# Weaving the sparse-attention indexer of blocks 1 to 3 into the feed-forward stage ahead of it, in a decoder-layer kernel on Trainium2

## The chip, the core and the metric

The kernel runs on one core of a Trainium2 chip. A core has five engines with a program each: PE (TensorE, matmuls), DVE (VectorE), ACT (ScalarE), POOL (GpSimd) and SP (SyncE, which issues the DMAs here). They run side by side and meet only at semaphores. The metric is the device time of one execution in microseconds (us), as the median of several.

## The reference

One decoder layer over 2048 prompt tokens and 64 sample tokens: RMSNorm and a combined projection; group A, sparse attention in which an indexer picks for each query its 256 best keys; group B, gated linear attention (GLA); an output projection; a SwiGLU feed-forward. What the change touches:

```python
# the indexer: a score for each query t and key s, from 8 index heads
dots  = jnp.einsum('bqhd,bsd->bqhs', iqs, idx_keys)
score = jnp.einsum('bqh,bqhs->bqs', iws, jax.nn.relu(dots))
score = jnp.where(key_pos <= tp, score, -jnp.inf)
_, sel = lax.top_k(score, topk)                  # topk = 256
# softmax attention over the picked keys gives attn_o
mix = jnp.concatenate([attn_o, gla_o], axis=-1)
x = x + jnp.einsum('btc,cd->btd', mix, w_out_l)
h = rmsnorm(x, ffn_g)
u = jax.nn.silu(jnp.einsum('btd,df->btf', h, wg)) * jnp.einsum('btd,df->btf', h, wu)
x = x + jnp.einsum('btf,fd->btd', u, wd)
```

D_MODEL is 1024, D_FF is 2816, and a head has 64 dimensions.

## The kernel before, in words

The 2048 prompt tokens are four blocks of 512 tokens, and a block is four tiles of 128 queries (tiles 0 to 15); the sample tokens are a fifth block. `SCHED` lists the stages, and every engine walks through it in its own program: P (projection), G (GLA), I (indexer), F (output projection and feed-forward), A (attention). The order is P0 G0 I0 A0, and then for b = 1 to 4: P(b) G(b) I(b) F(b-1) A(b), and F4 at the end. So block b's indexer stands just ahead of the feed-forward of block b-1, and the search for its top 256 keys runs on DVE while PE does that feed-forward.

**Stage I(b).** The scores of a tile are made in units: one index head and one chunk of up to 512 keys (`IU`). PE multiplies (two matmuls, lines 768 and 770, into one of 8 PSUM banks), ACT takes the relu (line 1142), DVE multiplies by the query's weight and adds to the row of scores (lines 1575 and 1577). Blocks 1, 2 and 3 have 64, 96 and 128 units. POOL then masks the diagonal (line 1852).

**The search.** The 256th largest score of each query is found bit by bit in 32 steps (`search_step`): a comparison with a running count for each tile (line 1344), then two small instructions for all tiles of the step (1347, 1350). `end_search` counts and ranks ties and turns the scores into an additive mask, in six instructions for each chunk of 512 keys (lines 1358 to 1376). A step takes all four tiles of the block at once. Some steps (`early_steps`) stand ahead of the norm in F, the rest behind it (`pick_block`). Tiles 2 and 3 alone are searched inside attention A0 (`late_picks`).

**Stage F(b).** O: 8 accumulations of 24 matmuls (the output projection, for one 128-row piece of the residual each) and the sum of squares for the norm. U: 44 accumulations of 24 matmuls (gate and up, in turn). D: 8 outputs of 66 matmuls. Weights come in fp32, and are split into two fp16 halves by ACT (`highs`, lines 1000 and 1002) and by POOL or DVE (`lows`, lines 1754 and 1312) into a ring of four tiles. In O ACT copies each result out of PSUM and POOL adds it to X (lines 1239, 1900). Between O and U the norm goes through ACT (970 to 974, 1249, 1253), DVE (1300 to 1306, 1608) and POOL (1906). U's products are put together by POOL (`gated`).

**Stage A(b).** For each tile and head (a unit, 32 in a block): logits on PE (810, 812), mask and maximum on DVE (1631, 1634), exp on ACT (1167), transposes and the product with V on PE (824, 835), scaling on DVE (1640, 1644). PE's `logits` runs one unit ahead and waits for DVE's mask after three banks. DVE gets to the first mask of A(b) only when it is through with the search; POOL waits for DVE's end of F.

The functions that the diff touches, and what calls them:

## Time and profile before

| what | us |
|---|---|
| median of 3 runs | 4000.27 (3999.38 to 4002.51) |
| the profiled execution | 4002.26 |
| its span in the trace | 4000.4 |
| PE busy | 3288.3 (82% of the span) |
| DVE busy | 2147.4 (54%) |
| ACT busy | 1824.1 (46%) |
| POOL busy | 1720.6 (43%) |

The profile is of one execution. Its stages, by PE's instructions, in us from the start of the span:

| block b | end of P(b) | first dots of I(b) | first accumulation of U in F(b-1) | end of D in F(b-1) | first mask of A(b) on DVE |
|---|---|---|---|---|---|
| 1 | 623.1 | 678.1 | 797.4 | 1148.0 | 1149.6 |
| 2 | 1422.6 | 1476.8 | 1620.6 | 1973.6 | 1975.3 |
| 3 | 2302.5 | 2357.5 | 2528.5 | 2881.2 | 2913.3 |

A busy share is an average over stages. What a change is worth is read from the stage in which it stands: from which engine was the last to be ready there.

### The profile page before, as it was taken

Reading aid. Unit: us, or ns where it says so; the run is one execution under the profiler, and the core shown is the slowest. Engines: PE = TensorE matmul, PEld = TensorE weight load, DVE = VectorE, ACT = ScalarE, POOL = GpSimd, SP = SyncE. Lnnn points to the kernel's source line nnn. Section 1 sums busy time; section 2 is a strip of 40 time slices with the busy share of each in tenths; the row PEclk is TensorE's granted clock in tenths of the full one; section 3 lists DMA queues with packets and bytes.
Section 4 is the critical chain, followed back from the end, with each engine's and each line's share of the span. In section 5 each row is a group of like instructions: output and inputs, shape, how many; then the busy total and the mean of one; then the engine's idle time right before and its main releaser. Section 6 shows DMA issues by size and latency. Waiting matters only on the chain.

```text
span 4000.4 us, 57257 instructions
## 1 busy us (share of the span) xinstructions
PE 3288.3 (82%) x19950; PEld 1844.1 (46%) x19950; DVE 2147.4 (54%) x3923; ACT 1824.1 (46%) x2702; POOL 1720.6 (43%) x1292
## 2 busy tenths in 40 slices
PE   3972597699989978799989968799879866999865
PEld 1451445244447452344476532344367742444455
DVE  3625663799115638899244648899944411100155
ACT  1331234555445346554464346554355514554356
POOL 2014202578654024676542033676621014776434
PEclk9995699899989999899999989899989957999766
DMA  2301031223220311232210201232210252232356
GB/s 84 93 25 42 6 98 36 63 89 105 85 86 30 99 35 58 74 100 82 76 64 22 93 27 53 69 105 85 78 35 1 96 157 93 90 103 83 104 188 217
DMA packets 112068, 313.08 MB, mean 78 GB/s; under 512 B 14035, under 2 KB 20515, under 8 KB 111747
## 3 DMA queue, kind: packets, MB, share of 16 engines
q1 hardware_dynamic: 111874, 310.63, 24.7%
q8 instruction: 106, 1.74, 0.2%
q14 instruction: 88, 0.71, 0.1%
HBM read 296.35 MB, written 14.24 MB: 78 GB/s over the span
## 4 chain that ended last, share of the span: by engine, by line
PE 58%; DVE 17%; issue 8%; ACT 5%; POOLq 4%; DMA 3%; POOL 2%; DVEq 2%; ACTq 0%; SPq 0%
PE bank L585 15%; PE bank L586 15%; PE bank L587 15%; DVE spare L1344 7%; PE bank L835 5%; PE bank L824 2%; DVE scores L1577 2%; DVE ring L1312 1%; ACT ring L1000 1%; DVE R L1631 1%; DMA kT<-in_w_gu 1%; ACT bank L1142 1%; POOL H L1906 1%; DVE miss L1347 1%; PE bank L810 1%
## 5 line engine op out<-in xcount | busy, mean ns | idle before, releaser
L585 PE MATMUL bank<-H,ring 128*128 128x512 f16 (+2 forms) x2560 | 855.2, 351 | 145.3 <-POOL H L1906 92.8
L586 PE MATMUL bank<-H,ring 128*128 128x512 f16 (+2 forms) x2560 | 855.1, 351 | 0.0
L587 PE MATMUL bank<-H,ring 128*128 128x512 f16 (+2 forms) x2560 | 854.4, 350 | 0.0
L1344 DVE TENSOR_SCALAR_CACHE_REDUCE spare<-scores,cand 128x640 uint8<-128x640 f32 (+4 forms) x448 | 662.5, 1479 | 43.5 <-issue 3.6
L1754 POOL TENSOR_TENSOR ring<-raw,ring 128x1024 f16<-128x1024 f32 (+1 forms) x252 | 488.2, 1942 | 290.1 <-ACT raw L1002 284.5
L1000 ACT ACTIVATE ring<-raw 128x1024 f16<-128x1024 f32 (+2 forms) x356 | 348.9, 980 | 386.2 <-PE bank L587 159.4
L585 PEld LDWEIGHTS bank<-H,ring 128*128 128x128 f16 (+1 forms) x2560 | 259.6, 102 | 407.6 <-issue 140.3
L587 PEld LDWEIGHTS bank<-H,ring 128*128 128x128 f16 (+1 forms) x2560 | 261.0, 103 | 246.5 <-issue 8.2
L586 PEld LDWEIGHTS bank<-H,ring 128*128 128x128 f16 (+1 forms) x2560 | 260.2, 102 | 242.8 <-issue 6.6
L1631 DVE CUSTOM_DVE_ANT_0 R<-bank,scores 128x512 f32<-128x512 f32 (+3 forms) x256 | 140.8, 592 | 383.1 <-PE bank L812 371.6
L585 PE MATMUL bank<-R,ring 128*128 128x512 f16 (+1 forms) x880 | 298.1, 354 | 37.8 <-POOL R L1927 25.6
L1264 ACT ACTIVATE mixA<-bank 128x512 f32<-128x512 f32 (+1 forms) x220 | 114.4, 520 | 464.4 <-PE bank L587 464.2
L835 PE MATMUL bank<-vtok,R 128*128 128x128 f32 x2176 | 286.1, 289 | 23.7 <-DVE R L1644 22.1
L586 PE MATMUL bank<-R,ring 128*128 128x512 f16 (+1 forms) x880 | 297.9, 354 | 0.0
L587 PE MATMUL bank<-R,ring 128*128 128x512 f16 (+1 forms) x880 | 297.7, 354 | 0.0
L835 PEld LDWEIGHTS bank<-vtok,R 128*128 128x128 f32 x2176 | 274.1, 205 | 27.1 <-issue 19.9
L1312 DVE SCALAR_TENSOR_TENSOR ring<-raw,ring 128x1024 f16<-128x1024 f32 x104 | 134.1, 1293 | 253.4 <-ACT ring L1000 252.3
L1178 ACT ACTIVATE R<-bank 128x512 f32<-128x512 f32 (+3 forms) x320 | 156.8, 530 | 196.8 <-PE bank L824 196.4
L1002 ACT ACTIVATE raw<-raw 128x1024 f32<-128x1024 f32 (+1 forms) x252 | 237.6, 943 | 0.0
L1000 ACT ACTIVATE ring<-kT 128x1024 f16<-128x1024 f32 (+2 forms) x189 | 181.1, 963 | 113.5 <-PE bank L587 69.1
L810 PE MATMUL bank<-kT,q 128*128 128x256 f16 (+3 forms) x384 | 128.8, 340 | 123.0 <-DVE mx L1631 95.3
L824 PE MATMUL bank<-cst,R 128*128 128x128 f32 x1088 | 166.4, 291 | 71.5 <-ACT R L1167 65.5
(299 smaller groups left out, 6013.8 us busy)
## 6 DMA issues: line engine op xcount, KB each, us to landing
raw<-in_w_gu SPq DMA_DIRECT2D x132, 512.0 KB, 3.6
raw<-in_w_in SPq DMA_DIRECT2D x104, 512.0 KB, 3.5
kT<-in_w_gu SPq DMA_DIRECT2D x88, 512.0 KB, 3.8
raw<-in_w_d SPq DMA_DIRECT2D x48, 384.0 KB, 3.1
X<-in_xT SPq DMA_DIRECT2D x8, 2048.0 KB, 9.3
raw<-in_w_d SPq DMA_DIRECT2D x48, 320.0 KB, 3.2
raw<-in_w_out SPq DMA_DIRECT2D x24, 512.0 KB, 3.5
kT<-in_w_d SPq DMA_DIRECT2D x32, 384.0 KB, 3.2
```

The costliest lines, as they stand in the source:

```text
L585: mm(o, lhs[0], rhs[0], start=first, stop=False)
L586: mm(o, lhs[0], rhs[1], start=False, stop=False)
L587: return mm(o, lhs[1], rhs[0], start=False, stop=last)
L810: mm(bank[n % 3][:, 0:kn], q[:, h, cq:cq + 128], kT[:, h // 4, 0, k0:k0 + kn], start=True, stop=False)
L824: last = nc.tensor.transpose(bank[3 + n % 2][:, 128 * (t % 4):128 * (t % 4) + 128], lg[:, u % 2, 128 * t:128 * t + 128], ident)
L835: last = mm(bank[5 + u % 2][:, 0:128], pT[:, u % 2, t, :], vtok[:, t, :], start=(t == 0), stop=(t == i))
L1000: last = A(ring[:, n % 4, 0, 0:cols], whole[:, 0:cols], ACT.Copy, scale=W_UP)
L1002: last = A(whole[:, 0:cols], whole[:, 0:cols], ACT.Copy, scale=W_UP)
L1312: v.scalar_tensor_tensor(ring[:, n % 4, 1, 0:cols], raw_at(n)[0][:, 0:cols], W_UP, ring[:, n % 4, 0, 0:cols], ALU.mult, ALU.subtract).then ...
L1344: v.tensor_scalar(flags[:, 0:128 * (i + 1)], row_of(i), cut_at[:, i % 4:i % 4 + 1], None, ALU.is_ge, ALU.add, accum_out=tally[:, i % 4:i % ...
L1631: v.tensor_tensor_reduce(lg[:, u % 2, k0:k0 + kn], bank[n % 3][:, 0:kn], m, 1.0 / Q_SCALE, OUTSIDE, ALU.add, ALU.max, mx[:, u % 2, c:c + 1 ...
L1754: g.tensor_tensor(ring[:, n % 4, 1, 0:cols], raw_at(n)[0][:, 0:cols], ring[:, n % 4, 0, 0:cols], ALU.subtract).then_inc(S("w_split"), 1)
```

## The change

For b = 1 to 3 the stage I(b) is gone from `SCHED`. Its units are spread over the accumulations of F(b-1), which is then called woven: a slot is one accumulation of O (8 slots) or U (44 slots), and behind each of the first slots stand three units (`I_NEXT`, `i_slot`), so that the 64, 96 and 128 units reach up to slot 21, 31 and 42. PE makes their dots behind the slot's accumulation (`dots_for`), now with 4 banks instead of 8; ACT takes the relu (`relus_for`), DVE adds (`adds_for`). O and the sum of squares move to banks 4 to 6. The loops over U are written out for this.

The output projection starts right after GLA. Its first four weight tiles are split in the projection stage (`p_ahead`). X is loaded when PE is through with G. DVE now adds the product to X itself and splits O's weights, and applies the gain together with the norm; ACT's copies and POOL's adds in O are gone. U's first accumulation takes its eight pieces of H one by one (`f_h` counts pieces).

The search takes two tiles at a time, then the other two; in block 3 two, one, one. A group's first step may stand only five slots after the one behind which its last unit was added. A plan with fixed costs (`SLOT_US`, `UNIT_PE_US`, `UNIT_DVE_US`, and a cost for each step) says how many steps stand behind each slot; what is left of the search follows after the last slot. Tile 15 gets 16 of its 32 steps there; the other 16 and its `end_search` stand between the units of A3. Stores of keys and values move into P, and some buffers get another place.

```diff
-EARLY_NS = 38000
-LATE_TILES = [2, 3]
+LATE_TILES = [2, 3, 15]
+LATE_STEP = 16
+SLOT_US, UNIT_PE_US, UNIT_DVE_US = 5.2, 0.43, 0.75
...
-            SCHED += [("P", b), ("G", b), ("I", b), ("F", b - 1), ("A", b)]
+            SCHED += [("P", b), ("G", b)] + [("I", b)] * (b == NBLK) + [("F", b - 1), ("A", b)]
...
+        I_NEXT = [{u: min(n0 + 3 * (u + 1), n1) for u in range(-1, KT + 36)}
+                  for n0, n1 in ((sum(i < 4 * b for i, _, _ in IU), sum(i < 4 * b + 4 for i, _, _ in IU))
+                                 for b in range(1, NBLK))]
+        def i_slot(b, slot):
+            return range(I_NEXT[b][slot - 1], I_NEXT[b][slot]) if slot < KT + 36 else range(0)
...
+            def dots_for(b, slot):
+                for n in i_slot(b, slot):
+                    i, c, h = IU[n]
+                    k0, kn = score_chunks(i)[c]
+                    cq = 128 * (i % 4)
+                    pe.wait_ge(S("i_added"), n - 3)
+                    mm(bank[n % 4][:, 0:kn], iq[:, h, cq:cq + 128], ikT[:, 0, k0:k0 + kn], start=True, stop=False)
+                    mm(bank[n % 4][:, 0:kn], iq[:, h, cq:cq + 128], ikT[:, 1, k0:k0 + kn], start=False, stop=True
+                       ).then_inc(S("i_dots"), 1)
...
+                    if woven(b):
+                        sp.wait_ge(S("end_pe"), nph)
+                        load_x(b, NT)
...
+                    for s in range(2 * NF if woven(b) else 0):
+                        w = weights_at(base["U", b] + s)
+                        pe.wait_ge(S("u_bank_free"), u0 + s + 1)
+                        for k in range(KT):
+                            if s == 0:
+                                pe.wait_ge(S("f_h"), KT * b + k + 1)
+                            last = three(bank[4 + s % 4][:, 0:NT], [w[e][:, 128 * k:128 * k + 128] for e in range(2)],
+                                         [H[:, e, k, 0:NT] for e in range(2)], k == 0, k == KT - 1)
+                        last.then_inc(S("products"), 1)
+                        dots_for(b, KT + s)
...
+            def search(b):
+                t = list(tiles_of(b))
+                groups = [t[0:2], t[2:4]] if b < NBLK - 1 else [t[0:2], t[2:3], t[3:4]]
+                for tiles in groups:
+                    done = max(n for n, u in enumerate(IU) if u[0] == tiles[-1]) + 1
+                    yield done, 0
+                    dve.wait_ge(S("i_diag"), tiles[-1] - 1)
+                    late = b == NBLK - 1 and tiles[-1] in LATE_TILES
+                    for n in range(LATE_STEP if late else STEPS):
+                        search_step(tiles, n)
+                        yield done, sum(128 * (i + 1) / 960 + 0.35 for i in tiles) + 0.5
+                    if not late:
+                        end_search(tiles)
+                        yield done, sum(128 * (i + 1) / 960 * 6 for i in tiles)
...
+                if kind == "F" and woven(b):
+                    start_search(tiles_of(b + 1))
+                    dve.wait_ge(S("x_in"), 16 * x_loads(nph))
+                    for dt in range(KT):
+                        dve.wait_ge(S("products"), base["O", b] + dt + 1)
+                        v.scalar_tensor_tensor(X[:, dt, :], bank[4 + dt % 2][:, :], 1.0 / (W_UP * M_UP), X[:, dt, :],
+                                               ALU.mult, ALU.add).then_inc(S("o_added"), 1)
+                        lows(base["O", b] + dt + 4)
+                        adds_for(b, dt)
+                    dve.wait_ge(S("f_root"), b + 1)
+                    newton(nF[0], nF[1], nF[2], nF[3], H_UP)
...
+                    for s in range(2 * NF):
+                        units = i_slot(b, KT + s)
+                        adds_for(b, KT + s)
+                        credit = min(credit + SLOT_US + (UNIT_PE_US - UNIT_DVE_US) * len(units), 2 * SLOT_US)
+                        while credit > 0 and I_NEXT[b][min(KT + s - 5, KT + 35)] >= ready:
+                            ready, cost = next(picks, (10 ** 6, 0))
+                            credit -= cost
+                    for _ in picks:
+                        pass
```

How the rows of the programs move, at the places that matter. First DVE's program of **before**, at the end of I3 and the start of the search for block 3 (tiles 12 to 15; a row is a line, an operation, what it writes and reads, its shape and how many in a row):

```order
L1575 TENSOR_SCALAR scores<-bank,iw 128x512
L1577 SCALAR_TENSOR_TENSOR scores<-bank,iw,scores 128x512 x7
L1337 MEMSET cand 128x4
L1344 TENSOR_SCALAR spare,tally<-scores,cand 128x1664
L1344 TENSOR_SCALAR spare,tally<-scores,cand 128x1792
L1344 TENSOR_SCALAR spare,tally<-scores,cand 128x1920
L1344 TENSOR_SCALAR spare,tally<-scores,cand 128x2048
L1347 TENSOR_SCALAR miss<-tally 128x4
L1350 SCALAR_TENSOR_TENSOR cand<-miss,cand 128x4
```

And the **changed** program of DVE around its first search step of block 3 (line 1465 or 1467 is an add, 1421 a comparison, 1424 and 1427 the two small ones):

```order
L1465 TENSOR_SCALAR scores<-bank,iw 128x512
L1421 TENSOR_SCALAR spare,tally<-scores,cand 128x1664
L1421 TENSOR_SCALAR spare,tally<-scores,cand 128x1792
L1424 TENSOR_SCALAR miss<-tally 128x2
L1427 SCALAR_TENSOR_TENSOR cand<-miss,cand 128x2
L1421 TENSOR_SCALAR spare,tally<-scores,cand 128x1664
L1421 TENSOR_SCALAR spare,tally<-scores,cand 128x1792
L1424 TENSOR_SCALAR miss<-tally 128x2
L1427 SCALAR_TENSOR_TENSOR cand<-miss,cand 128x2
```

Before, the first step follows the last of the 128 units. Now it follows unit 80 of 128 (behind the 19th accumulation of U), has half the tiles, and 47 more adds stand between the steps that follow.

On PE, the **changed** program at one of the slots of U (606 to 608 are the accumulation's matmuls, 627 and 628 the dots):

```order
L607 MATMUL bank<-H,ring 128x512
L608 MATMUL bank<-H,ring 128x512
L627 MATMUL bank<-ikT,R 128x512
L628 MATMUL bank<-ikT,R 128x512
L627 MATMUL bank<-ikT,R 128x512
L628 MATMUL bank<-ikT,R 128x512
L627 MATMUL bank<-ikT,R 128x512
L628 MATMUL bank<-ikT,R 128x512
L606 MATMUL bank<-H,ring 128x512
```

**Before**, the last dots of I3 stand directly ahead of the first matmuls of the output projection, and none stands in U:

```order
L768 MATMUL bank<-ikT,R 128x512
L770 MATMUL bank<-ikT,R 128x512
L768 MATMUL bank<-ikT,R 128x512
L770 MATMUL bank<-ikT,R 128x512
L585 MATMUL bank<-mixA,ring 128x512
L586 MATMUL bank<-mixA,ring 128x512
L587 MATMUL bank<-mixA,ring 128x512
```

On DVE in A3 the **changed** program has steps for tile 15 between the units (1748 and 1751 are a unit's mask and maximum, 1757 and 1761 the scaling):

```order
L1748 ISA R,mx<-bank,R 128x256
L1748 ISA mx 128x1
L1751 TENSOR_REDUCE nmax<-mx 128x1
L1757 RECIPROCAL rden<-den 128x1
L1761 TENSOR_SCALAR R<-bank,rden 128x64
L1421 TENSOR_SCALAR spare,tally<-scores,cand 128x2048
L1424 TENSOR_SCALAR miss<-tally 128x1
L1427 SCALAR_TENSOR_TENSOR cand<-miss,cand 128x1
L1748 ISA R,mx<-bank,scores 128x512
```

There are 16 such steps over the first 23 units of A3, and `end_search` for tile 15 stands behind the last of them, with the mask of unit 23 ahead of it and the mask of unit 24 behind it. The program of before has none of these.

## Rows read from the trace of the kernel before

**Rows 1.** Windows over U and D of F2, the gap and A3; busy us.

```profile
core 0: us, PE busy (x) PEld busy (x) DVE busy (x) ACT busy (x) POOL busy (x), PEclk, DMA share, GB/s
2528.50:2759.40 230.90, 230.86 (x1056) 103.97 (x1056) 218.82 (x227) 117.70 (x138) 166.84 (x106) 0.99 0.29 93
2759.40:2881.20 121.80, 116.69 (x529) 52.23 (x528) 115.62 (x120) 46.41 (x66) 79.02 (x54) 0.97 0.32 92
2881.20:2913.30 32.10, 1.37 (x7) 0.51 (x6) 28.88 (x46) 0.60 (x1) 3.94 (x4) 0.57 0.00 0
2913.30:3180.90 267.60, 234.65 (x1894) 196.13 (x1895) 109.84 (x419) 154.77 (x243) 50.19 (x75) 0.95 0.09 31
```

**Rows 2.** Windows from the end of the search to attention, blocks 1 and 2.

```profile
1015.10:1148.00 132.90, 127.75 (x583) 57.18 (x581) 0.01 (x1) 50.40 (x72) 80.74 (x60) 0.97 0.32 92
1918.90:1974.00 55.10, 54.73 (x254) 24.62 (x252) 0.00 (x0) 21.95 (x33) 35.18 (x26) 1.00 0.35 102
```

**Rows 3.** PE's timeline from GLA to I3: start, us, instruction, idle before.

```profile
2344.43 3.70 PE L751 MATMUL bank<-H,cst 128*128 128x512 f32 x8 [2.68 <-ACT H L1125]
2357.45 0.58 PE L768 MATMUL bank<-ikT,R 128*128 128x512 f16 x1 [9.32 <-ACTq L1291]
```

**Rows 4.** The page's DMA issues: size and us to landing of X.

```profile
X<-in_xT SPq DMA_DIRECT2D x8, 2048.0 KB, 9.3
```

**Rows 5.** Timeline of the norm between O and U in F2.

```profile
2517.63 10.58 POOL L1906 TENSOR_TENSOR H<-R,H 128x512 f16<-128x512 f32 x8 [10.54 <-ACT H L1253]
2528.54 0.61 PE L585 MATMUL bank<-H,ring 128*128 128x512 f16 x1 [21.10 <-POOL H L1906]
```

**Rows 6.** Groups by shape in I3: count, busy us, mean ns, idle before.

```profile
L1577 DVE SCALAR_TENSOR_TENSOR scores<-bank,iw,scores 128x512 f32<-128x512 f32 x91 | 68.3, 751 | 9.1 <-ACT bank L1142 0.9
```

**Rows 7.** DVE groups by shape in block 3's search (2462 to 2914).

```profile
L1344 DVE TENSOR_SCALAR_CACHE_REDUCE spare<-scores,cand 128x2048 uint8<-128x2048 f32 x32 | 75.1, 2346 | 3.1
L1344 DVE TENSOR_SCALAR_CACHE_REDUCE spare<-scores,cand 128x1664 uint8<-128x1664 f32 x32 | 62.3, 1946 | 2.9
L1347 DVE TENSOR_SCALAR miss<-tally 128x4 int32<-128x4 f32 x32 | 26.9, 839 | 2.5
L1344 DVE DVE_READ_ACCUMULATOR spare<-scores,cand 128x1 f32 x128 | 10.7, 84 | 0.0
L1350 DVE SCALAR_TENSOR_TENSOR cand<-miss,cand 128x4 int32<-128x4 int32 x32 | 5.2, 163 | 2.4
```

**Rows 8.** DVE groups by shape in block 2's search (1554 to 1919).

```profile
L1350 DVE SCALAR_TENSOR_TENSOR cand<-miss,cand 128x4 int32<-128x4 int32 x32 | 21.0, 656 | 2.4
L1347 DVE TENSOR_SCALAR miss<-tally 128x4 int32<-128x4 f32 x32 | 15.4, 480 | 2.5
```

**Rows 9.** DVE groups by shape in A0 (318 to 492), with its late search.

```profile
L1350 DVE SCALAR_TENSOR_TENSOR cand<-miss,cand 128x1 int32<-128x1 int32 x64 | 13.1, 204 | 5.5 <-issue 0.8
L1347 DVE TENSOR_SCALAR miss<-tally 128x1 int32<-128x1 f32 x64 | 9.8, 154 | 4.9
```

**Rows 10.** All 160 instances of line 1347: duration ns min/median/max, first and last start.

```profile
L1347 DVE TENSOR_SCALAR miss<-tally x160: 153/170/1895, 321.0 to 2815.6; 128x4 int32<-128x4 f32 x96, 128x1 int32<-128x1 f32 x64
```

**Rows 11.** Windows over `end_search` of blocks 1, 2 and 3.

```profile
946.50:1015.10 68.60, 68.60 (x320) 31.09 (x319) 65.72 (x57) 36.41 (x43) 59.12 (x34) 1.00 0.28 91
1837.90:1918.90 81.00, 75.16 (x339) 33.48 (x338) 76.79 (x81) 28.79 (x43) 53.00 (x34) 0.96 0.30 82
2817.10:2912.80 95.70, 65.47 (x304) 29.37 (x301) 89.96 (x105) 24.48 (x35) 48.41 (x31) 0.86 0.22 64
```

**Rows 12.** DVE's timeline at the end of block 3's `end_search`, POOL silent.

```profile
2908.09 0.69 DVE L1376 SCALAR_TENSOR_TENSOR scores<-spare,scores 128x512 f32<-128x512 f16 x1
2912.05 0.69 DVE L1376 SCALAR_TENSOR_TENSOR scores<-spare,scores 128x512 f32<-128x512 f16 x1
```

**Rows 13.** DVE's timeline in A3: the first mask of a unit.

```profile
3051.64 0.69 DVE L1631 CUSTOM_DVE_ANT_0 R<-bank,scores 128x512 f32<-128x512 f32 x1 [4.63 <-PE bank L812]
```

**Rows 14.** A window just after the start of A3.

```profile
2918.00:2922.00 4.00, 3.01 (x13) 2.62 (x14) 0.31 (x3) 2.54 (x5) 0.72 (x1) 0.50 0.00 0
```

265 lines of the change are left out of this document (162 added, 103 removed).

## The prediction

> **What bounds the kernel now.** I read the windows by stage first, since the busy shares of the page mix stages with different limits. U and D of F2 are PE's: 230.9 and 121.8 us long, with PE busy for 230.86 and 116.69 of them [rows 1]. 44 accumulations in 230.9 us make 5.25 us each, and 1056 matmuls make 0.22 us each. At the end of D the blocks differ. In blocks 1 and 2 DVE is through with its search 132.9 and 55.1 us before attention starts, and PE is the last [rows 2]. In block 3 it is the other way round: between 2881.2 and 2913.3 PE does next to nothing and DVE is busy for 28.88 of 32.10 us [rows 1]. So the search has a slack of 133 us in block 1, 55 in block 2, and none (minus 32) in block 3. The change takes time out of PE's path and delays the search, so the question is which of the two arrives last at the start of A1, A2 and A3. I count both from the first dots of I(b), as before has them: 678, 1477 and 2357.5.
>
> **PE's path.** GLA ends on PE at 2344.4 + 3.7 = 2348.1, and the next matmul waits until 2357.45 for ACT [rows 3]. The first O accumulation now fills this gap (5.25 us; I add 1 us for the four weight tiles that are split at the end of the projection). Only then come dots, from 2358.5. A unit is two matmuls, 0.44 us, so a full slot is 5.25 + 1.3 = 6.55 us. X is asked for only when GLA is over on PE and lands 9.3 us later [rows 4], and DVE's first adds queue behind X and behind a weight split; PE then waits some 4 us for bank 0. With 8 sums of squares at 0.9 us the last sum is done at about 2416.5. Between it and U's first accumulation stands the norm: PE waits 21.1 us, the last 10.58 of them for POOL's eight subtractions [rows 5]. Now U starts after the first of these, and its first accumulation lasts as long as they do, so the second starts at about 2439. That is 81.5 us behind the old first dots; I use this for all three blocks (before, the second accumulation of U starts at 2533.8).
>
> From there 43 accumulations take 226 us, and the units that stand in U from its second slot on (37, 69, 101) take 16, 30 and 43 us. DVE's lumps of steps hold PE back a little in the slots with units (a slot's units wait for the adds of the slot before): I take 10 us. With D at 121.8 us, D ends at 678 + 81.5 + 226 + 16 + 10 + 121 = 1132 (before 1148), at 1477 + 81.5 + 226 + 30 + 10 + 122 = 1947 (before 1973.6) and at 2357.5 + 81.5 + 226 + 43 + 10 + 122 = 2840 (before 2881.2). PE alone would gain 16, 27 and 41 us, and block 3's gap of 32 on top.
>
> **DVE's path.** The group rule decides. The first pair's last unit is number 32, 48 and 64 of the block; three in a slot and five slots of distance put the first step behind slot 15, 20 and 26, which is U's accumulation 7, 12 and 18 (counted from 0). At 6.55 us a slot, and 1.5 us for relu and add, the search starts at 807, 1639 and 2557. Before, it started at 731, 1554 and 2462, just behind the last unit: it is 76 to 95 us later, and 16, 33 and 47 units still have to be added among the steps. A 512-wide add is 0.751 us [rows 6], with gaps 0.8 to 0.84: 13, 26 and 40 us. Where the steps run in between, DVE waits for nothing, so what it has to do simply adds up:
>
> A comparison takes 1.946 us for 1664 keys and 2.346 for 2048, with 0.084 for the count's read and 0.1 of gaps [rows 7]: 0.133 us for each 128 keys and 0.4. The two small instructions cost 0.839 + 0.163 in block 3 [rows 7] and 0.656 + 0.480 in block 2 [rows 8], with gaps 1.16 and 1.29 us a step; in A0, where POOL does little, 0.204 + 0.154 [rows 9], with gaps 0.52. They don't get cheaper with two tiles, and there are now 64 (block 3: 80) instead of 32 in a block. `end_search` of a whole block took 68.6, 81.0 and 95.7 us [rows 11]; with POOL silent a chunk of 512 keys takes 3.96 us [rows 12], about 6 otherwise.
>
> Block 1: adds 13, steps 32 x (2.27 + 1.29) = 114 and 32 x (2.80 + 1.29) = 131, ends 69: 327 us, from 807 to 1134. This meets PE at 1132.
> Block 2: adds 26, steps 32 x (3.33 + 1.29) = 148 and 32 x (3.86 + 1.29) = 165, ends 81: 420 us, from 1639 to 2059. After 1947 POOL is silent: 14 steps at 0.77 us less and a cheaper second end (28 for 41) give back 24; POOL's thinner load in the longer slots another 5. So 2030.
> Block 3: adds 40, 32 steps of tiles 12 and 13 at 4.4 + 1.16 = 178, their end 55: 273 us, to 2830; tile 14: 3 steps at 3.55 and 29 at 2.93, to 2925; its end 4 x 3.96 + 2.7 = 19, to 2944; 16 steps of tile 15 at 2.53 + 0.52, to 2993. Less 5 for POOL's thinner load: 2988.
>
> **Attention.** A(b) starts with the later of the two: A1 at 1133 instead of 1149 (-16), A2 at 2030 instead of 1975.3 (+55), A3 at 2988 instead of 2913.3 (+75). Inside A3 DVE waits 4.63 us in a unit for PE's logits [rows 13], so a step of 3.05 us hides in it. `end_search` for tile 15 does not: 2.4 + 0.3 + 16 = 19 us in one unit, and PE runs only one unit ahead. Less the 4.6 of idle time: +14. If the steps did not hide, they would cost up to 49 more; if PE's lead hid the end too, 0. In the I stages that go, ACT, POOL and SP have nothing on the path that sets the end: their work is hidden by PE's slots of 6.55 us (ACT has 117.70 us in 44 of U's slots [rows 1], 2.7 us each, and three relus more, each no longer than an add).
>
> The clock adds little. In A3's first microseconds it was 0.50, which is the lower level of 1.2 GHz, after 32 us without matmuls [rows 14]; A2 now starts after a gap too, and half speed over the 4 us of that row costs 2 us.
>
> **Sum.** -16 + 55 + 75 + 14 + 2 = +130, against the profiled execution's 4002.3 (span 4000.4): 4132. The median of the runs is 2 us lower than that execution: 4130.
>
> **A rule that bears on the sum.** The small TENSOR_SCALAR of line 1347 took between 153 and 1895 ns, with a median of 170 [rows 10], the long ones beside POOL's work. The Trainium skill, page "SBUF — State Buffer", section "Who interferes with whom", says that a VectorE tensor_scalar in a 2-port mode and a GpSimd instruction exclude each other, the later one waiting for the whole of the other, whereas the form that writes its accumulator doesn't take part. This speaks against splitting the search into more steps. By the rule's worst case each step beside POOL waits for a whole instruction of it, which is the upper bound of the next sentence; by its best case, lucky order, none does, which is rival A.
> By rows alone: 50 steps of block 2 and 35 of block 3 lie beside POOL, and between the mean (0.48 to 0.84) and the longest (1.895) there is 1.4 and 1.06 us each, +108. To the other side, with POOL's cover gone (0.52 a step and 3.96 a chunk), block 2 would be 38 + 13 us shorter and block 3 22 + 18: -91. I take the means, since DVE met the same engine in the same stage.
>
> **Rivals.**
> A. Steps and ends at their quiet price (0.52 us, 3.96 a chunk), because the woven slots let DVE and POOL pass each other. A2 starts at 1979, A3 at 2948: 4039. For it: POOL's share of U falls from 166.84 of 230.9 us [rows 1], 0.72, to 0.60 with longer slots. Against it: 0.60 is nearer to 0.72 than to silence. 8%.
> B. Faster: DVE keeps up, and PE's D is last in every block. That gives -16, -28, -73 at the starts and +14 in A3: 3897. It is decided at one place: block 3's search has to be over by 2840, 283 us after its start, against 431 of work; it would need steps before unit 64's slot plus five, which the program doesn't have, or adds that run much earlier than PE's slots. 4%.
> C. The steps in A3 don't hide, since PE's wait of three banks is shorter than a step, and each costs its 3.05 us; or the first of the lumps hold PE longer in U: 16 x 3.05 = +49, 4179. For it: DVE's 109.84 us in A3 [rows 1] would grow by 68, and PE, busy for 234.65 of 267.6, has little room of its own. Against it: the 4.63 us of idle time [rows 13]. 10%.
> D. No change that a measurement can tell (0.2%, 8 us, is about the limit): block 2 and 3 lose no more than block 1 and the stage I give back. Nothing in the rows leads there. 2%.
>
> **How the numbers follow.** The forecast has 76%, with 4095 to 4165 as its own range (10 us on each of three DVE paths, and A3's end between 0 and 25). The range for 8 in 10 reaches down towards A and up to C: 4060 to 4180. Faster by over 0.2%: B alone, 4%. Within: 2%. Slower: the rest, 94%.
>
> **What would show it.** The profile after should have: the second accumulation of U 82 us behind the old place of the first dots; the first comparison of a block at U's accumulation 7, 12, 18; no gap of PE before A1, one of about 83 us before A2 and one of about 148 before A3, with DVE busy in both; line 1424 at a mean over 0.4 us while POOL works and under 0.2 in the gaps; in A3 DVE's idle time before the mask gone in 16 units, PE's waits unchanged there, and one stall of about 15 us at tile 15's `end_search`. I am wrong if the gaps are missing, if DVE idles while a search is open, or if U's slots are much longer than 6.6 us.

## The result and the profile after

| | before | after |
|---|---|---|
| median of 4 runs, us | 4001.39 (3999.38 to 4004.81) | 4148.02 (4137.35 to 4178.49) |
| ratio of the means, 95% interval | | 1.0378 (1.032 to 1.0436) |
| profiled execution, span | 4002.3, 4000.4 | 4178.49, 4176.0 |

The changed kernel is slower by 3.8%, inside the range (4060 to 4180) and 18 us above the forecast of 4130; the profiled execution, the slowest of the four, lies just inside too. The stages of the profiled execution after, as the table of before has them:

| block b | end of P(b) | start of U's second accumulation in F(b-1) | first comparison | end of D in F(b-1) | first mask of A(b) on DVE |
|---|---|---|---|---|---|
| 1 | 644.2 | 799.2 | 844.9 | 1165.5 | 1167.1 |
| 2 | 1440.3 | 1581.2 | 1660.2 | 1981.1 | 2047.4 |
| 3 | 2371.3 | 2528.3 | 2644.2 | 2926.3 | 3060.4 |

The windows of after (start:end, length, then busy us of PE, PEld, DVE, ACT and POOL, PE's granted clock, DMA) are in order: the gap before A2; stage G of block 3; U of F2 from its first dots (they stand behind the first accumulation, 0.3 us ahead of the second) to its last; D of F2; the gap before A3; and the masks of A3.

```profile
1981.10:2047.40 66.30, 1.16 (x7) 0.51 (x6) 60.31 (x95) 0.60 (x1) 4.04 (x4) 0.53 0.00 0
...
2383.80:2430.70 46.90, 37.49 (x162) 30.93 (x162) 12.25 (x38) 4.92 (x11) 0.00 (x0) 0.50 0.00 1
2528.00:2757.80 229.80, 220.60 (x1026) 99.05 (x1025) 141.22 (x191) 133.29 (x207) 135.18 (x88) 0.99 0.23 77
2809.60:2926.30 116.70, 116.67 (x528) 52.19 (x528) 109.23 (x128) 44.55 (x63) 74.82 (x51) 0.98 0.32 92
2926.30:3060.40 134.10, 1.36 (x7) 0.52 (x6) 121.75 (x191) 0.60 (x1) 3.70 (x4) 0.52 0.00 0
3060.40:3321.90 261.50, 213.15 (x1572) 176.23 (x1573) 158.49 (x490) 137.17 (x212) 47.19 (x70) 0.91 0.04 14
```

Against [rows 1]: the gap of 32 us before A3 has become one of 134, and block 2, which had none [rows 2], has one of 66. In both PE and POOL do next to nothing, and DVE is busy for over nine tenths: the search is what the others wait for. Block 1 has no gap (1165.5 to 1167.1). The masks of A3 took 231.6 us before and take 261.5 now.

**The account.** The two profiled executions differ by 176 us. One part is the clock of stage G, between the projection and the indexer. Its state updates, a chain of small float32 matmuls, took 30.4 us in all four blocks of before, at a granted clock of 1.00. In after they took 46.9 us in blocks 0, 1 and 3, at 0.50, and 32.8 in block 2, at 0.89, since the clock rose to 1.00 inside it. That is 3 x 16.5 + 2.4 = 52 us. I take it out by counting, for each block, the time from the end of P(b) to the first mask of A(b), less what G(b) took over 30.4 us:

| from the end of P to attention, less G's excess | block 1 | block 2 | block 3 | masks of A3 | G's excess, blocks 0 to 3 |
|---|---|---|---|---|---|
| before | 526.5 | 552.7 | 610.8 | 231.6 | 0 |
| after | 506.4 | 604.7 | 672.6 | 261.5 | 51.9 |
| difference | -20 | +52 | +62 | +30 | +52 |

The sum is 176. The same numbers are given below for each experiment, since the profiled execution shows in which blocks G ran at half clock, and the other runs behind a median don't.

### The profile page after: what moved, and what is told of

Its sections match the earlier page's. It is cut to its first block, busy times and chain, and to the rows that moved or that the text cites. A ratio compares the mean times of both kernels' runs of the same rounds, so it can differ in the third digit from the quotient of the medians.

```text
span 4176.0 us, 56774 instructions
## 1 busy us (share of the span) xinstructions
PE 3331.4 (80%) x19950; PEld 1900.8 (46%) x19950; DVE 2283.0 (55%) x4243; ACT 1721.2 (41%) x2591; POOL 1624.7 (39%) x1232
## 4 chain that ended last, share of the span: by engine, by line
PE 53%; DVE 25%; issue 8%; ACT 4%; DMA 3%; POOLq 3%; DVEq 2%; POOL 2%; ACTq 1%; SPq 0%
PE bank L606 12%; PE bank L608 12%; PE bank L607 12%; DVE spare L1421 12%; PE bank L867 4%; PE bank L856 2%; DVE ring L1389 2%; DVE miss L1424 2%; DVE scores L1467 2%; DVE cand L1427 1%; DVE R L1748 1%; DMA kT<-in_w_gu 1%; ACT ring L1054 1%; POOL H L2032 1%; DVE spare L1446 1%
## 5 line engine op out<-in xcount | busy, mean ns | idle before, releaser
L1421 DVE TENSOR_SCALAR_CACHE_REDUCE spare<-scores,cand 128x640 uint8<-128x640 f32 (+8 forms) x448 | 662.3, 1478 | 41.5 <-issue 1.8
L1871 POOL TENSOR_TENSOR ring<-raw,ring 128x1024 f16<-128x1024 f32 (+1 forms) x216 | 411.8, 1910 | 299.2 <-ACT raw L1056 293.3
L1389 DVE SCALAR_TENSOR_TENSOR ring<-raw,ring 128x1024 f16<-128x1024 f32 x140 | 200.5, 1435 | 348.2 <-ACT ring L1054 347.1
L1998 POOL TENSOR_TENSOR R<-scores,near_bias 128x256 f32<-128x256 f32 (+1 forms) x128 | 92.2, 722 | 490.1 <-DVE nmax L1751 217.6
L1467 DVE SCALAR_TENSOR_TENSOR scores<-bank,iw,scores 128x512 f32<-128x512 f32 (+3 forms) x252 | 172.2, 683 | 153.9 <-ACT bank L1070 135.3
```

The source lines that it names most:

```text
L1389: v.scalar_tensor_tensor(ring[:, n % 4, 1, 0:cols], raw_at(n)[0][:, 0:cols], W_UP, ring[:, n % 4, 0, 0:cols], ALU.mult, ALU.subtract).then ...
L1421: v.tensor_scalar(flags[:, 0:128 * (i + 1)], row_of(i), cut_at[:, i % 4:i % 4 + 1], None, ALU.is_ge, ALU.add, accum_out=tally[:, i % 4:i % ...
L1467: v.scalar_tensor_tensor(out, bank[n % 4][:, 0:kn], w, out, ALU.mult, ALU.add).then_inc(S("i_added"), 1)
L1871: g.tensor_tensor(ring[:, n % 4, 1, 0:cols], raw_at(n)[0][:, 0:cols], ring[:, n % 4, 0, 0:cols], ALU.subtract).then_inc(S("w_split"), 1)
```

## The experiments

The first four and the last two are edits of the kernel after; the diffs show the lines that matter, with `...` for what is left out. Of each profiled execution the numbers of the table above are given in its order: blocks 1 to 3, the masks of A3, G's excess.

### The fourth O tile at the start of F

```diff
-                        if u < len(TILES) and u + 4 < p_ahead(b):
+                        if u < len(TILES) and u + 4 < min(p_ahead(b), len(TILES) + 3):
...
+                    if woven(b):
+                        highs(base["O", b] + 3, "dve")
...
                     start_search(tiles_of(b + 1))
+                    lows(base["O", b] + 3)
```

> The changed kernel, but only three of the output projection's weight tiles are split at the end of the projection; the fourth is split at the start of F. Theory: in the changed kernel the fourth split stands between projection and GLA, PE pauses some 3 us there instead of 1, and GLA then runs at a granted clock of 0.50 (47 us instead of 30 between first and last state update) in some blocks. Then G1, G2 and G3 should be back at a clock near 1.00 and 30 us, and the median at 4095 to 4130. Rival: GLA's clock has to do with something else (the moved buffers, or the position in time): two or three of the four G stages stay at 47 us and the median stays at 4140 or above.

In after, ACT and DVE split O's fourth weight tile between P and G, and DVE gives PE its start only then. PE's first matmul behind the projection waits 3.09 us:

```profile
644.70 1.05 ACT L1054 ACTIVATE ring<-raw 128x1024 f16<-128x1024 f32 x1
645.78 1.22 DVE L1389 SCALAR_TENSOR_TENSOR ring<-raw,ring 128x1024 f16<-128x1024 f32 x1 [4.13 <-ACT ring L1054]
647.26 0.58 PE L716 MATMUL bank<-cst,X 128*128 128x128 f32 x2 [3.09 <-DVEq L1851]
```

and in before 0.86 us:

```profile
623.97 0.41 PE L684 MATMUL bank<-cst,X 128*128 128x128 f32 x2 [0.86 <-ACTq L1291]
```

Measured: 4120.7 us (4110.84 to 4130.14), ratio 1.0279 (1.0246 to 1.0313); profiled 4126.0. Blocks 505.3, 599.8, 669.0; masks of A3 261.1; G's excess 16.5, all of it in block 1. PE's pause was 0.86 us again, and blocks 2 and 3 had G at 30.4 us. But block 1 had it at 46.9, behind the short pause:

```profile
633.40:680.30 46.90, 37.49 (x162) 30.94 (x162) 12.27 (x38) 4.85 (x11) 0.00 (x0) 0.50 0.00 1
1426.80:1457.20 30.40, 20.19 (x162) 17.01 (x162) 12.30 (x38) 4.86 (x11) 0.00 (x0) 1.00 0.00 1
```

So the place of the tile by itself is worth 1 to 5 us in each block. The half-clock stages were fewer in this execution, one for three, but the short pause doesn't rule them out.

### Half of the search left out

```diff
-                    for n in range(LATE_STEP if late else STEPS):
+                    for n in range(LATE_STEP if late else STEPS // 2):
```

Sixteen of the 32 search steps are left out in every woven group but tile 15's.

> The changed kernel with 16 instead of 32 search steps for tiles 4 to 14 (half of the bit search is left out). Theory: DVE's search alone sets the start of A2 and A3; in the changed kernel A2 starts 66 us and A3 134 us behind the end of PE's D. 16 steps less of each group take 156 and 145 us from DVE, so both gaps close, A1 moves by under 5 us, and the median is near 4148 - 66 - 134 = 3948 (3930 to 3975). Rival: PE is held back inside the slots by relu, adds or weight splits as well; then D itself ends later than 122 us after a U of 44 slots and the median stays above 4000.

Measured: 3964.95 us (3954.26 to 3973.02), ratio 0.9899 (0.9866 to 0.9933). Blocks 506.3, 539.6, 562.8; masks of A3 262.6; G's excess 5.2. The gap before A2 is gone. The one before A3 is down from 134 us but still 26, where both were expected to close:

```profile
1945.60:1947.40 1.80, 0.82 (x6) 0.44 (x6) 0.01 (x1) 0.60 (x1) 0.88 (x1) 1.00 0.00 0
2809.90:2836.30 26.40, 1.38 (x7) 0.51 (x6) 23.37 (x36) 0.60 (x1) 3.71 (x4) 0.58 0.00 0
```

Nothing on PE's side was changed, so the 65 us of block 2 and 110 of block 3 were the search. The 110 are less than the 145 expected, since of the work that was left more lay beside POOL and cost more: in block 3's search a line of `end_search` (1448, on 512 keys) took 1660 ns where it takes 961 in after. This kernel also shows what PE alone has gained by the weaving: 13 us in block 2, where I had worked out 27.

### Four units in a slot

```diff
-        I_NEXT = [{u: min(n0 + 3 * (u + 1), n1) for u in range(-1, KT + 36)}
+        I_NEXT = [{u: min(n0 + 4 * (u + 1), n1) for u in range(-1, KT + 36)}
```

> The changed kernel with four units in a slot instead of three. Theory: the end of the search is its start plus DVE's work, and the start is set by the slot of the first pair's last unit plus five. With four units that slot is 11 instead of 15 in block 2 and 15 instead of 20 in block 3; the first step then stands behind slot 16 instead of 20, and 20 instead of 26. At about 7 us a slot A2 starts 20 to 28 us earlier, A3 30 to 40 us, A1 within 10 us, median 4080 to 4105. Rival: four banks are too few for four units in a slot, PE waits for adds in each slot, and what is won at the start is lost in the slots: median within 15 us of the changed kernel.

Measured: 4122.19 us (4118.78 to 4131.27), ratio 1.0285 (1.026 to 1.031). Blocks 509.7, 592.9, 660.6; masks 263.3; G's excess 33.0. Counted from the end of P, with G's excess taken out, the search starts 10, 18 and 27 us earlier than in after (174.4, 199.9 and 229.7 against 184.2, 217.5 and 256.4). Attention starts 3 us later, 12 and 12 us earlier. The gaps are still 62 and 118 us. The median lies above the expected 4080 to 4105 and below the rival's 4133 and more.

The earlier start reaches attention in part only, since the search itself grew longer: from 387.2 to 393.0 us in block 2 and from 416.2 to 430.9 in block 3. The adds are not the reason. Fewer of them stand beside the search than in after (28 for 33 in block 2, 44 for 47 in block 3). Two other sums grew: in block 3 DVE's small instructions (lines 1424 and 1427) took 56.4 us instead of 41.8, and in block 2 `end_search` took some 11 us more. In both blocks POOL was busy for longer while the search ran. The windows over block 3's search, in after and in this kernel:

```profile
2644.20:3060.40 416.20, 269.04 (x1217) 118.75 (x1215) 382.62 (x511) 129.18 (x187) 178.54 (x121) 0.83 0.18 56
```

```profile
2584.60:3015.50 430.90, 298.43 (x1353) 131.58 (x1351) 397.60 (x508) 142.39 (x201) 203.70 (x136) 0.85 0.20 61
```

That POOL's work sets this price is shown by the ninth experiment.

### Only block 1 woven

```diff
-LATE_TILES = [2, 3, 15]
+EARLY_NS = 38000
+WOVEN = (0,)
+LATE_TILES = [2, 3]
...
-            SCHED += [("P", b), ("G", b)] + [("I", b)] * (b == NBLK) + [("F", b - 1), ("A", b)]
+            SCHED += [("P", b), ("G", b)] + [("I", b)] * (b - 1 not in WOVEN) + [("F", b - 1), ("A", b)]
```

> Only block 1's indexer is woven (into F0); blocks 2 and 3 have their I stages back, tile 15 is searched with its block, with the buffers and stores of the changed kernel. Theory: block 1 is the one block in which PE and DVE finish together, so A1 starts about 16 us earlier relative to the end of P1 if GLA runs at full clock, and 4 us earlier if not; A2 and A3 start as before, 55 and 32 us from their old places behind PE and DVE. Median 3980 to 4000. Rival: the loss sits in something that all blocks share (moved buffers, stores in P, longer code): then A2 and A3 are late here too and the median is above 4030.

Measured: 3989.3 us (3977.41 to 4017.69, 10 runs), ratio 0.9953 (0.9935 to 0.9972). Blocks 506.3, 550.1, 609.6; masks 233.0. The profiled execution is the slowest of the ten (4017.69), with G's excess at 35.4 us. The gain of block 1, 20 us, stands alone and in full. A1 and A2 have no gap, and A3 has one of 33 us as in before:

```profile
1165.50:1167.10 1.60, 0.66 (x6) 0.49 (x6) 0.00 (x0) 0.60 (x1) 0.69 (x1) 1.00 0.00 0
1988.80:1990.50 1.70, 0.76 (x5) 0.42 (x6) 0.00 (x0) 0.60 (x1) 0.83 (x1) 1.00 0.00 0
2896.30:2929.20 32.90, 1.35 (x6) 0.52 (x6) 29.67 (x48) 0.60 (x1) 4.24 (x4) 0.56 0.00 1
```

### The late tile alone

No block is woven (stages I1 to I3 are back); tile 15 is late. Against the kernel of the fourth experiment:

```diff
-WOVEN = (0,)
+WOVEN = ()
-LATE_TILES = [2, 3]
+LATE_TILES = [2, 3, 15]
```

> The kernel after with the weaving taken out of all three blocks (stages I1 to I3 are back, as before), but with block 3's tile 15 out of the search from step 16 on: its 16 steps and its end stand in A3's units. My theory: A3 starts when PE's D is over and no longer when DVE's search is, 32 us earlier than the kernel before (2881 for 2913), and A3 itself grows by 30 us as it did in the kernel after (10 from steps beside the weight splits, 19 from the end of the search in one unit): no change, 3990 to 4010. Rival 1: the growth of A3 in the kernel after came from elsewhere (the half clock after a gap of 134 us): then A3 grows by less than 10 and the kernel takes 3975 to 3985. Rival 2: with DVE later than PE by more than the steps taken out, A3 starts only 10 us earlier: 4015 to 4030.

Measured: 4010.9 us (4004.53 to 4032.44, 10 runs), ratio 1.0019 (1.0001 to 1.0037). Blocks 529.4, 552.6, 582.2; masks 265.2; G's excess 18.8 in the profiled execution. A3 starts 28.6 us earlier and its masks take 33.6 us longer. The median is 0.9 us above the expected 3990 to 4010. My theory held in both of its halves, and both rivals fell. The half clock behind a long gap is no cause, since A3 starts without a gap here:

```profile
2906.60:2908.30 1.70, 0.80 (x4) 0.42 (x5) 0.04 (x1) 0.60 (x1) 0.88 (x1) 1.00 0.00 0
2908.30:3173.50 265.20, 214.99 (x1576) 177.25 (x1574) 158.54 (x490) 137.36 (x212) 50.13 (x73) 0.91 0.04 14
```

### The late tile spread out

The edit is to the kernel of the fifth experiment.

```diff
-LATE_STEP = 16
+LATE_STEP = 20
...
+                            units = [u for u in range(last - parts + 1) if u not in WEIGHT_UNITS]
+                            for n, u in enumerate(units):
+                                plan[u] = (i, range(LATE_STEP + (STEPS - LATE_STEP) * n // len(units),
+                                                    LATE_STEP + (STEPS - LATE_STEP) * (n + 1) // len(units)), None)
+                            for p in range(parts):
+                                plan[last - parts + 1 + p] = (i, range(0), p)
```

> As e5_late_tile_only, but tile 15 leaves the search at step 20, its 12 late steps keep out of the units in which weight tiles are split, and its end is cut in five parts, one in each of five units. By my theory the 10 and the 19 us of A3 go, and the start of A3 stays some 31 us earlier: A3 within 8 us of its length before, 3972 to 3982. Rival: DVE has no idle time in A3 that a step can use without holding PE (PE's lead is one unit), and each step costs its 3 us wherever it stands: 12 x 3 + 20 = 56 us in A3, 4020 to 4030.

Measured: 3981.35 us (3976.75 to 3988.28), ratio 0.994 (0.9921 to 0.9959). Blocks 526.3, 552.8, 581.3; masks 239.3; no excess of G. PE's waits for DVE's masks during A3, first of the kernel with the late tile in one piece, then of this one (us in total, times, longest):

```profile
PE bank L856 <- DVE mx L1784: 45.2, 29, 17.8
```

```profile
PE bank L856 <- DVE mx L1820: 23.6, 32, 2.8
```

The one wait of 17.8 us, `end_search` in one unit, is gone, and of the two waits of 5.8 us in units with a weight split each is 2.8 again. Twelve steps and the whole end cost A3 8 us instead of the rival's 56: they do hide in DVE's idle time, nearly all, if no unit gets more than it has room for. How much of the 26 us between the two kernels is the place of the steps and how much their number (12 for 16) was not tried apart.

### Block 1 woven and the late tile spread

Block 1 as in the fourth experiment, O's fourth tile as in the first, the late tile as in the sixth. Against the kernel of the sixth, beside the edits of the first:

```diff
-WOVEN = ()
+WOVEN = (0,)
```

> Three changes together: block 1's indexer woven into F0 as in e4_block1_only, the fourth O tile split at the start of F0 and not at the end of P1 as in e1_split, and tile 15 late as in e6_late_tile_spread. If the gains add up: 16 us from I1 (measured in e4_block1_only at A1), 24 to 30 from A3: 3950 to 3965. Rival: stage G falls to half clock in two or more blocks more often than in the kernel before, and takes 17 us a time back: 3970 to 3990.

Measured: 3953.03 us (3948.71 to 3956.39), ratio 0.9866 (0.9842 to 0.9889). Blocks 505.5, 552.4, 578.6; masks 239.2; no excess of G. The gains add up, and this kernel beats both: 1.3% below before.

```profile
2858.40:2860.10 1.70, 0.78 (x4) 0.42 (x5) 0.01 (x1) 0.60 (x1) 0.85 (x1) 1.00 0.00 0
2860.10:3099.30 239.20, 210.92 (x1575) 174.06 (x1573) 147.90 (x474) 137.19 (x212) 50.17 (x73) 0.96 0.05 15
```

### A longer pause ahead of G

```diff
+                    if 0 < b < NBLK:
+                        for _ in range(4):
+                            act.drain()
+                            A(spare[:, :], spare[:, :], ACT.Copy)
```

This is added to the kernel before.

> The kernel before with four copies of a spare tile onto itself, each behind a drain, added on ACT at the end of P1, P2 and P3: PE pauses about 2 to 3 us longer between P and G. In the kernel after the fourth O tile's split stands there, PE paused for 3.1 us instead of 0.86, and all of the next stage G ran at a granted clock of 0.50 (46.9 us instead of 30.4). My theory: the length of this pause decides at which level G runs, so G1 to G3 take 47 us in all or most blocks, and the kernel takes 3 x 17 + 3 x 2 = 57 us more where all three fall, 4020 at least. Rival: the clock of G doesn't hang on this pause: G stays at 30.4 or 32.8 us in most blocks and only the pause is added, at most 10 us, 4003 to 4012.

Measured: 4018.54 us (4012.24 to 4027.7, 10 runs), ratio 1.003 (1.0016 to 1.0043); profiled 4017.61. Blocks 531.1, 556.0, 615.5; masks 233.1; G's excess 2.4. PE paused for 3.64 us, more than in after, and still G ran at full clock in blocks 1 and 2:

```profile
627.22 0.41 PE L684 MATMUL bank<-cst,X 128*128 128x128 f32 x2 [3.64 <-ACTq L1295]
```

```profile
636.10:666.50 30.40, 20.19 (x162) 17.01 (x162) 12.29 (x38) 4.85 (x11) 0.00 (x0) 1.00 0.00 1
1438.20:1468.60 30.40, 20.19 (x162) 17.01 (x162) 12.27 (x38) 4.92 (x11) 0.00 (x0) 1.00 0.00 1
2321.50:2354.30 32.80, 22.80 (x162) 19.08 (x162) 12.28 (x38) 4.92 (x11) 0.00 (x0) 0.89 0.00 0
```

My theory, that the length of this pause decides, fell in this execution; the nine others have no trace. The rival's account is nearer, though the kernel lost 13.7 us where it allowed 10. The three blocks became 4.6, 3.3 and 4.7 us longer with G's excess out, which is 12.6 of the 13.7.

### POOL's part of the weight splits made thin

```diff
-                                lows(c + 2 * s + 4, i, 4, 128 * len(D_BLOCKS[2 * s]) if ahead == "D" else WT)
+                                lows(c + 2 * s + 4, i, 4, 8 if b < NBLK else WT)
...
-                                lows(c + 2 * s + 5, i, 4, 128 * len(D_BLOCKS[2 * s + 1]) if ahead == "D" else WT)
+                                lows(c + 2 * s + 5, i, 4, 8 if b < NBLK else WT)
```

> The kernel after, with POOL's part of the weight splits inside U of blocks 0 to 2 cut to 8 of 1024 columns (the low halves of these weights are not computed): POOL is busy for about 0.3 of U instead of 0.6, and nothing else changes on DVE or PE. My theory: the small instructions of a step and the ends of the searches cost more only because POOL works beside them, so the price of a step's small work falls about half way to its quiet price: some 20 us from the search of block 2, 15 to 20 from block 3, nothing from block 1 (PE is last there). A2 starts 15 to 25 us and A3 another 12 to 20 us earlier: 4100 to 4120. Rival: the long ones come from PE's or ACT's work or from DVE's own order; then the means of these lines stay and the kernel takes 4140 to 4155.

The edit reaches U of block 3's feed-forward too, which lies behind A3 and so outside the numbers below. The splits of D's weights at the end of U, 640 and 768 columns wide, keep their width.

Measured: 4105.43 us (4084.31 to 4109.64), ratio 1.0249 (1.0218 to 1.0279); profiled 4084.31. Blocks 500.8, 575.3, 668.8; masks 261.5; G's excess 5.1. Block 2 gained 29 us, block 1 and 3 only 6 and 4. The small instructions of the steps of block 2's first pair (count, busy us, mean ns, idle before), in after:

```profile
L1424 DVE TENSOR_SCALAR miss<-tally 128x2 int32<-128x2 f32 x32 | 25.9, 811 | 2.5
...
L1427 DVE SCALAR_TENSOR_TENSOR cand<-miss,cand 128x2 int32<-128x2 int32 x32 | 15.5, 483 | 2.4
```

and with the thin splits:

```profile
L1424 DVE TENSOR_SCALAR miss<-tally 128x2 int32<-128x2 f32 x32 | 11.6, 361 | 2.5
L1427 DVE SCALAR_TENSOR_TENSOR cand<-miss,cand 128x2 int32<-128x2 int32 x32 | 6.1, 191 | 2.4
```

1.29 us a step became 0.55, without any edit to DVE's work. Over the whole search of block 2 the two lines took 42.3 us instead of 64.5, and `end_search` some 6 us less: together the 29 us. So POOL's work is the cause of the price, and the rival (PE's or ACT's work, or DVE's own order) fell. In block 3 the same pair of lines cost 0.745 us a step in after, already little, and 0.62 here:

```profile
L1424 DVE TENSOR_SCALAR miss<-tally 128x2 int32<-128x2 f32 x32 | 14.0, 439 | 2.5
L1427 DVE SCALAR_TENSOR_TENSOR cand<-miss,cand 128x2 int32<-128x2 int32 x32 | 9.8, 306 | 2.8 <-issue 0.4
```

and what stands in the gaps behind D meets no POOL at all. The 15 to 20 us that I expected of block 3 were not there to be had.

### One group in blocks 1 and 2

```diff
-                groups = [t[0:2], t[2:4]] if b < NBLK - 1 else [t[0:2], t[2:3], t[3:4]]
+                groups = [t] if b < NBLK - 1 else [t[0:3], t[3:4]]
```

> The kernel after with one group of four tiles in blocks 1 and 2, and tiles 12 to 14 as one group in block 3: half as many small instructions, but the search can't start before unit 64 (block 1) or 96 (blocks 2 and 3) of the block and five slots more. By the starts and the step prices of the kernel after: block 1 starts at about 911 and ends at 911 + 32 x 6.3 + 69 = 1182, 16 us behind D; block 2 starts at about 1754 and ends 1754 + 32 x 8.4 + 60 = 2084, 37 us later than with pairs; block 3 starts at 2702 and ends 2702 + 254 + 50 + 49 = 3055, as with pairs. Sum: 50 to 55 us slower than the kernel after, 4190 to 4205. Rival: it is the doubled small instructions that made the kernel slow, not the late start; then one group ends earlier in blocks 2 and 3 by the 32 steps saved, 35 to 40 us each: 4080 to 4110.

Measured: 4127.98 us (4113.1 to 4148.28), ratio 1.0316 (1.0265 to 1.0367). Blocks 499.0, 597.9, 669.0; masks 261.3; G's excess 16.0. Counted as above, attention starts 7, 7 and 4 us earlier than in after. Both expectations fell, and the median lies between their ranges. In block 2 the start was 73 us later (290.9 us behind the end of P against 217.5), and the search 80 us shorter (307.0 us against 387.2). It had half as many small instructions (31.1 us against 64.5), no adds to share its time with (0 against 23.7), and more of it lay behind D, where POOL is silent (its `end_search` took some 14 us less). The late start and the shorter search cancel. Neither the split into pairs nor the start alone made the kernel slow.

What the steps cost PE can be read here. In block 2 this kernel's 23 slots of U from the second accumulation on, with three units and no steps, took 146.3 us, 6.36 each, with PE never idle. In after, where steps lie among them, the same 23 took 171.4 us, 7.45 each. Of the 25 us more, 17.4 are idle time, and the other 7.7 are PE's own work at a granted clock of 0.95 instead of 1.00. First this kernel, then after, then PE's waits for DVE's adds in after (us in total, times, longest, from 1660 to 1753):

```profile
1551.50:1697.80 146.30, 146.30 (x691) 67.49 (x690) 48.59 (x69) 90.04 (x142) 89.96 (x59) 1.00 0.25 80
```

```profile
1581.20:1752.60 171.40, 154.00 (x692) 67.42 (x691) 112.03 (x153) 91.97 (x142) 93.33 (x61) 0.95 0.22 71
```

```profile
PE bank L627 <- DVE scores L1467: 17.2, 12, 5.1
```

D ended 509.6 us behind the end of P here, 538.4 in after and 551.0 in before, with G's excess out. So in block 2 the weaving without steps in the slots gives PE 41 us, and the steps take 29 of them back.

## Why the prediction was right

The sum, against the profiled executions: forecast -16 + 55 + 75 + 14 + 2 = +130; measured -20 + 52 + 62 + 30 = +124, and 52 more from the clock of G. The sign, the place of both gaps and each term's engine were as forecast. That the two sums are only 6 us apart is luck in part: counted from the end of its P, A1, A2 and A3 started 4, 3 and 13 us earlier than forecast, and the inside of A3 was 16 us longer. The gaps of PE were forecast as 83 and 148 us and were 66 and 134: in block 2 mostly since D ended 14 us later than worked out, in block 3 since the search ended 13 us earlier. The 2 us for the clock at the start of A2 don't show: its masks took 172.5 us, and 175.7 before.

- **What bounds it.** DVE's search is last in blocks 2 and 3, PE in block 1. Shown by the half search (65 and 110 us off blocks 2 and 3, nothing off block 1) and by weaving block 1 alone.
- **PE's path.** U's second accumulation was forecast 136 us behind the end of P (81.5 behind the old dots). It came 138.5, 138.5 and 140.5 us behind, with G's excess out. (In before it started at 2536.5 and not at 2533.8, since its first matmuls ran at half clock; nothing was worked out from that number.) D's end was forecast 16, 27 and 41 us earlier; it came 20, 13 and 40 us earlier. The step that was off is that DVE's lumps of steps hold PE back "a little", taken as 10 us: in block 2 PE waited 17.2 us, its clock was 0.91 in the stretch of these waits (1660 to 1753), and the slots took 7.45 us instead of 6.6. Slots much longer than 6.6 us stood in the prediction's own list of signs of being wrong, and here the mechanism was right and its size too small. It cost nothing, since DVE was last.
- **Start of the search.** Forecast 47, 80 and 118 us behind U's second accumulation; measured 45.7, 79.0 and 115.9. The rule of five slots does what the prediction says.
- **The search's length.** Block 2: forecast 391 us from first comparison to attention, measured 387.2. Block 3: forecast 431, measured 416.2. A step's two small instructions were taken at 1.00 us from [rows 7]; they took 0.745 in the first pair (8 us less over 32 steps) and less still behind it. In block 2 they were taken at 1.14 [rows 8]; they took 1.29 in the first pair (5 us more over 32 steps) and 0.83 in the second, where the prediction, with its 14 quiet steps, comes to 0.80.
- **Inside A3.** Forecast +14, measured +30. The end in one unit was the larger part, as forecast; it made PE wait 17.85 us where I had 14:

```profile
3264.70 0.40 PE L842 MATMUL bank<-kT,q 128*128 128x256 f16 x1 [17.85 <-DVE mx L1748]
```

  The rest, 12 us, was given to nothing. That a step of 3.05 us hides in the 4.63 us of [rows 13] doesn't hold in two of the four units in which DVE also splits weights: PE waited 6.1 and 5.8 us there, where it waited 2.8 before.

```profile
3134.87 0.40 PE L842 MATMUL bank<-kT,q 128*128 128x256 f16 x1 [6.14 <-DVE mx L1748]
```

```profile
2983.32 0.28 PE L810 MATMUL bank<-kT,q 128*128 128x256 f16 x1 [2.75 <-DVE mx L1631]
```

  And PE's own work between the first and the last mask took 213.2 us at a granted clock of 0.91, where it took 209.6 at 0.96. DVE's idle time before masks fell from 96.3 us to 69.2, after and before:

```profile
DVE R L1748 <- PE bank L844: 69.2, 25, 5.9
```

```profile
DVE R L1631 <- PE bank L812: 96.3, 25, 5.2
```

  Rival C, 49 us for steps that don't hide, stays wrong; the sixth experiment has twelve steps and the end for 8 us.
- **Rival A**, the quiet price, is what a silent POOL would give. Thinning it brought 29 us of block 2, so the rival had the mechanism and the wrong condition: the woven slots by themselves don't let DVE and POOL pass each other (means of 811 and 483 ns).
- **What was missed.** The clock of G. The prediction put only 1 us on the four tiles split at the end of P. From the end of P to the first state update it took 2.3 to 3.1 us more in blocks 1 to 3. Stage G, whose work the change leaves as it is, ran at half clock three times in the profiled execution, and that was in no term of the sum. The profiled execution lies 46 us above the forecast for it (4178.5 against 4132) with these 52 us, and 6 below without; the median lies 18 above. In how many blocks the other three runs had it, no trace shows; so how much of the median's 18 us is this clock stays open.
- **The rule that was weighed.** Line 1424 took 152 to 2021 ns, with a median of 169:

```profile
L1424 DVE TENSOR_SCALAR miss<-tally x288: 152/169/2021, 342.2 to 3244.8; 128x2 int32<-128x2 f32 x80, 128x1 int32<-128x1 f32 x64
```

  and with POOL's splits thin 153 to 1546:

```profile
L1424 DVE TENSOR_SCALAR miss<-tally x288: 153/168/1546, 323.6 to 3154.8; 128x2 int32<-128x2 f32 x80, 128x1 int32<-128x1 f32 x64
```

  Both of these longest ones ended with a split of POOL that had started just ahead of them: the one of 2021 ns beside a split 1024 columns wide, the one of 1546 ns beside one of 768 columns, 1.64 us long. The first of them:

```profile
1698.01 2.12 POOL L1871 TENSOR_TENSOR ring<-raw,ring 128x1024 f16<-128x1024 f32 x1 [2.69 <-ACT raw L1056]
1698.13 2.02 DVE L1424 TENSOR_SCALAR miss<-tally 128x2 int32<-128x2 f32 x1
```

  The comparisons don't wait: that of 1664 keys took 1946 ns before [rows 7], and as much in after and with POOL thin:

```profile
L1421 DVE TENSOR_SCALAR_CACHE_REDUCE spare<-scores,cand 128x1664 uint8<-128x1664 f32 x32 | 62.3, 1946 | 3.3
```

  The Trainium skill, page "SBUF — State Buffer", section "Who interferes with whom", says that of a VectorE tensor_scalar in a 2-port mode and a GpSimd instruction the later one waits for the whole of the other, and the form that writes its accumulator stays out of it. The trace agrees on both counts (2021 ns until the split was over, 1946 for the comparison everywhere); in which mode the small instruction ran it doesn't show.

## What to carry to other kernels

Before work is woven into a stage, ask for each block which engine has slack at its end, and how much. Here DVE had 133 us of it in block 1, which took the weaving as a gain of 20 us; it had 55 in block 2 and none in block 3, and both lost. A search that starts earlier doesn't end earlier by as much, if more of it then lies beside the engine that makes it dear. Work that is made late for one engine's sake has to be followed on the engine that does it to the end of the stage. Work put into another engine's idle time hides if each portion is smaller than the idle time of its own unit: the same tile's end made PE wait 17.8 us in one unit, and in five units no wait was longer than 2.8.

## What the runs showed of the hardware

**The level of G.** G's first to last state update took 30.4 to 30.8 us at a granted clock of 1.00, or 46.9 at 0.50, or between 32.7 and 39.4 where the clock rose or fell inside it. Over the twelve profiled kernels (48 stages), by how long PE had paused at the end of the projection:

| PE's pause ahead of G | stages | 30.4 to 30.8 us | 32.7 to 39.4 us | 46.9 us |
|---|---|---|---|---|
| 0.85 or 0.86 us | 29 | 22 | 3 | 4 |
| 3.09 us | 16 | 3 | 8 | 5 |
| 3.64 us | 3 | 2 | 1 | 0 |

In before, block 1, the clock was 1.00 until about 625, just behind the end of the projection, and 0.50 from 627 to 633, while PE had short pieces of work and pauses; it was 1.00 again when the state updates began at 633.3. In after it was 0.50 from 648 on and stayed there until the updates were over, at 703.5. What decides between the two is open. A longer pause goes with more stages that are not at full clock (13 of 16 against 7 of 29), but the added pause of 3.64 us had none at half clock for the whole stage. And block 0, with the short pause, came out in three ways in six kernels whose programs are the same up to there: 46.9 us in after, 32.7 in the tenth experiment, and 30.4 in the first, second, third and ninth. The Trainium skill, page "TensorE: Matmul & The Clock Gate", Part 1, says that the window in which the chip looks at PE's activity runs free of the program, so that one kernel can come out differently from run to run. That agrees with block 0; no run here shows the window itself. For a reader of times it means that an execution can be 16.5 us longer for each such stage. The ten runs of the fifth experiment fall into seven from 4004.5 to 4013.0 us and three from 4031.5 to 4032.4; the one of these three that was profiled had 18.8 us of it.

**POOL's subtraction** on 8 columns instead of 1024 took 255 ns instead of 2127 (means of one shape in U of F1): a hundredth of the work, an eighth of the time.

```profile
L1871 POOL TENSOR_TENSOR ring<-raw,ring 128x8 f16<-128x8 f32 x38 | 9.7, 255 | 76.7 <-ACT raw L1056 76.7
```

**The price that POOL's work sets is not one number.** The same two lines beside the same engine cost 1.29 us a step in the first pair of block 2 and 0.745 in that of block 3, both in after. The block is not what decides: with four units in a slot block 3's first pair had 1.13 (587 and 540 ns). How the small instructions fall against POOL's may decide it; that was not tested.
